# Gated linear attention by pairs of 128 tokens in place of chunks of 64 with carried states

## The reference

```
log_a = log_sigmoid(a_low @ w_a_up + b_a) / 16
b = cumsum(log_a within a chunk of 64 tokens)
q_d = q * exp(b);  k_d = k * exp(-b);  k_t = k * exp(b_last - b);  decay = exp(b_last)
att = tril(q_d @ k_d^T) per chunk;  o_intra = att @ v
for each chunk:  o_inter = q_d @ state;  state = decay * state + k_t^T @ v
o = rmsnorm(o_intra + o_inter) * silu(z)
```

## Time and profile before

| what | value |
|---|---|
| timed runs, median of 3 | 985.37 us |
| profiled execution, first to last instruction (span) | 984.4 us |
| time around the span (985.37 less 984.4) | 1.0 us |
| PE busy | 977.1 us, 99% |
| PE weight loads, beside the products | 828.7 us, 84% |
| DVE busy | 682.6 us, 69% |
| ACT busy | 585.1 us, 59% |
| POOL busy | 66.2 us, 7% |

### The profile page before, as it was taken

One profiled execution on the slowest core, in us unless ns is written; L12 is line 12 of the kernel. 1 busy time (PEld: TensorE's weight loads), 2 busy tenths in 40 slices (PEclk: granted clock), 3 DMA queues, 4 the chain that ended last, 5 costly groups with the idle time before them and its releaser, 6 DMA issues.

```text
span 984.4 us, 13450 instructions
## 1 busy us (share of the span) xinstructions
PE 977.1 (99%) x5186; PEld 828.7 (84%) x5186; DVE 682.6 (69%) x1159; ACT 585.1 (59%) x1026; POOL 66.2 (7%) x80
## 2 busy tenths in 40 slices
PE   9999999999999999999999999999999999999997
PEld 6887888888888998888888888888888777988886
DVE  5887776655667889766556678778577355787564
ACT  6777755444547896654445476557766354685443
POOL 1323110000000241000000000000020000000000
PEclk9999999999999999999999999999999999999999
DMA  9753555554555445555645556445533543336551
GB/s 364 308 195 129 171 174 211 198 205 175 200 185 173 170 161 181 177 208 174 227 177 200 185 196 248 171 171 190 195 129 137 186 148 128 129 129 208 179 190 43
DMA packets 27119, 180.33 MB, mean 183 GB/s; under 512 B 2992, under 2 KB 3888, under 8 KB 6320
## 3 DMA queue, kind: packets, MB, share of 16 engines
q1 hardware_dynamic: 26336, 176.98, 50.3%
q0 software_dynamic: 288, 2.10, 0.6%
q10 hardware_dynamic: 432, 0.39, 0.1%
HBM read 178.41 MB, written 1.05 MB: 182 GB/s over the span
## 4 chain that ended last, share of the span: by engine, by line
PE 99%; DMA 1%; DVE 0%; ACT 0%; SPq 0%; issue 0%; DVEq 0%
PE bank L340 25%; PE bank L295 16%; PE bank L297 16%; PE bank L296 16%; PE bank L348 13%; PE bank L310 1%; PE bank L470 1%; PE bank L486 1%; PE bank L591 1%; PE bank L520 1%; PE bank L311 1%; PE bank L531 1%; DMA front<-in_front 1%; PE bank L462 1%; PE bank L706 0%; PE bank L722 0%
## 5 line engine op out<-in xcount | busy, mean ns | idle before, releaser
L1357 DVE TENSOR_TENSOR lo<-raw,hi 128x1024 fp32r<-128x1024 f32 x318 | 375.9, 1228 | 20.0 <-ACT hi L837 20.0
L837 ACT ACTIVATE hi<-raw 128x1024 fp32r<-128x1024 f32 x318 | 320.2, 1050 | 96.9 <-PE bank L297 95.1
L340 PE MATMUL bank<-X,hi 128*128 128x512 f32 x1016 | 267.0, 395 | 0.0
L340 PEld LDWEIGHTS bank<-X,hi 128*128 128x128 f32 x1016 | 185.0, 189 | 33.2 <-issue 0.4
L348 PEld LDWEIGHTS bank<-X,lo 128*128 128x128 f32 x1016 | 138.5, 190 | 10.1
L348 PE MATMUL bank<-X,lo 128*128 128x256 f32 x1016 | 141.6, 282 | 0.0
L868 ACT ACTIVATE bt<-bank 128x256 f32<-128x256 f32 x135 | 51.0, 380 | 142.7 <-PE bank L340 134.3
L1371 DVE TENSOR_TENSOR zr<-bank,bt 128x256 f32<-128x256 f32 x64 | 27.1, 424 | 109.0 <-ACT bt L868 109.0
L295 PE MATMUL bank<-hi,zh 128*128 128x512 f32 x256 | 100.0, 391 | 0.0
L297 PE MATMUL bank<-hi,zl 128*128 128x512 f32 x256 | 99.8, 390 | 0.0
L296 PE MATMUL bank<-lo,zh 128*128 128x512 f32 x256 | 99.6, 389 | 0.0
(11 more groups left out here) (344 smaller groups left out, 1428.3 us busy)
## 6 DMA issues: line engine op xcount, KB each, us to landing
raw<-in_w SPq DMA_DIRECT2D x64, 1024.0 KB, 4.7
raw<-in_rin SPq DMA_DIRECT2D x8, 1024.0 KB, 4.7
raw<-in_wk SPq DMA_DIRECT2D x4, 1024.0 KB, 11.0
raw<-in_wq SPq DMA_DIRECT2D x4, 1024.0 KB, 9.4
raw<-in_wo SPq DMA_DIRECT2D x4, 1024.0 KB, 4.7
raw<-in_mk SPq DMA_DIRECT2D x4, 1024.0 KB, 4.8
raw<-in_mv SPq DMA_DIRECT2D x4, 1024.0 KB, 4.7
raw<-in_rout SPq DMA_DIRECT2D x4, 1024.0 KB, 4.8
```

The source lines that it names most:

```text
L340: return PE.matmul(bank[b][:, :], wh[:, c:c + P], x[:, k_, :, :].rearrange("p a b -> p (a b)"), start=k_ == 0, stop=k_ == NC - 1, skip_gro ...
L837: ACTE.activation(hi[u_ % HIS][:, c], raw[u_ % RAW][:, c], ACT.Copy).then_inc(hi_cut, 1)
L1357: DVE.tensor_tensor(lo[u_ % RAW][:, c], raw[u_ % RAW][:, c], hi[u_ % HIS][:, c].bitcast(F32), ALU.subtract).then_inc(lo_cut, 1)
```

## The change

The heads are worked in two halves of 128 tokens (the two rows of partitions) in place of four chunks of 64. The running sum starts anew every 128 tokens. The exponentials are taken relative to the sum at the middle of the half (token 63 of it), passed as a per-partition bias of the activation. The second half's tokens see the first half by one more score block (`gax`, 128 by 128), made from keys scaled to the first half's end and queries scaled from the second half's start. There are no states, no turned keys and no products on part of the array. PE does for a head: `g_first(n)`, three products of 128 columns; tile `ta` n; `g_second(n)`, three products of 256 columns; tile `wd` n. ACT makes six exponentials of 128 tokens for a head in place of two of 256 and copies the third score block; DVE makes two small scaled copies of the middles and ends, splits one scaling into halves, and masks the scores in two instructions that leave out one quarter, which two clears before the loop set to zero.

```diff
-            done = fill(("gkt", n), 1)
-            for j in range(2):
-                m = PE.transpose(bank[1][:, j * P:(j + 1) * P], gk[:, n, j * P:(j + 1) * P], ident[:, :])
-            m.then_inc(done, 1)
-        def g_states(n):
...
-            for c in (0, 2, 1):
-                r, j = (c % 2) * 64, c // 2
-                m = PE.matmul(bank[2 + c % 2][:, j * 256:j * 256 + 256], ktT[n % 2][r:r + 64, j, :],
-                              gv[r:r + 64, j, n * 256:(n + 1) * 256], start=True, stop=True, skip_group_check=True)
...
+            done = fill(("gax", n), 1)
+            PE.matmul(bank[1][:, 0:P], gk[:, n, 0:P], gk[:, n, P:S], start=True, stop=True).then_inc(done, 1)
...
-            for j in range(2):
-                PE.matmul(bank[3][:, j * 256:j * 256 + 256], at[n % 2][:, j, :], v_[:, j, :], start=j == 0, stop=False,
-                          skip_group_check=True)
-            for c in (2, 1, 3):
-                r, j = (c % 2) * 64, c // 2
-                m = PE.matmul(bank[3][r:r + 64, j * 256:j * 256 + 256], q_[:, c * 64:c * 64 + 64], st[c - 1][:, :],
-                              start=False, stop=True, skip_group_check=True)
+            PE.matmul(bank[3][:, 0:256], a_[:, 0, :], v_[:, 0, :], start=True, stop=False, skip_group_check=True)
+            PE.matmul(bank[3][:, 256:512], a_[:, 1, :], v_[:, 1, :], start=False, stop=False, skip_group_check=True)
+            PE.matmul(bank[3][:, 256:512], a_[:, 2, :], v_[:, 0, :], start=False, stop=True, skip_group_check=True).then_inc(done, 1)
...
             g_first(n)
             tokens("ta", n, X, (4, 5))
-            g_states(n)
+            g_second(n)
             tokens("wd", n, Y, (6, 7))
-            g_second(n)
...
-            ACTE.activation(tmp[n % 2][:, :], gb[:, n, :], ACT.Exp, scale=1.0 / 16).then_inc(ep_made, 1)
-            ACTE.activation(tmp[2 + n % 2][:, :], gb[:, n, :], ACT.Exp, scale=-1.0 / 16).then_inc(en_made, 1)
+            for j in range(2):
+                r = slice(j * P, (j + 1) * P)
+                i = ACTE.activation(tmp[n % 2][:, r], gb[:, n, r], ACT.Exp, scale=1.0 / 16, bias=dec[:, 1, n, 2 * j:2 * j + 1])
+            i.then_inc(ep_made, 1)
+            for j in range(2):
+                r = slice(j * P, (j + 1) * P)
+                i = ACTE.activation(tmp[2 + n % 2][:, r], gb[:, n, r], ACT.Exp, scale=-1.0 / 16, bias=dec[:, 0, n, 2 * j:2 * j + 1])
+            i.then_inc(en_made, 1)
+            ACTE.activation(sq[2 + n % 2][:, 0:P], gb[:, n, 0:P], ACT.Exp, scale=-1.0 / 16, bias=dec[:, 0, n, 1:2])
+            ACTE.activation(sq[2 + n % 2][:, P:S], gb[:, n, P:S], ACT.Exp, scale=1.0 / 16).then_inc(ex_made, 1)
...
-            ACTE.activation(ktT[n % 2][:, :, :], bank[1][:, 0:S].rearrange("p (a b) -> p a b", a=2),
-                            ACT.Copy).then_inc(freed[1], 1)
+            ACTE.activation(at[n % 2][:, 2, :], bank[1][:, 0:P], ACT.Copy).then_inc(freed[1], 1)
...
-            DVE.tensor_tensor_scan(gb[:, n, :], reset[:, :], u[:, :], 0.0, ALU.mult, ALU.add).then_inc(sum_made, 1)
+            step(DVE.tensor_tensor_scan(gb[:, n, :], reset[:, :], u[:, :], 0.0, ALU.mult, ALU.add))
+            own()
+            DVE.tensor_scalar(dec[:, 0, n, :], gb[:, n, 63:S:64], 1.0 / 16, None, ALU.mult)
+            DVE.tensor_scalar(dec[:, 1, n, :], gb[:, n, 63:S:64], -1.0 / 16, None, ALU.mult).then_inc(sum_made, 1)
...
-            d.wait_ge(ep_made, n + 1)
-            step(DVE.tensor_copy(dec[:, n, :], ep[:, 63:S:64]))
...
+            step(DVE.scalar_tensor_tensor(out=gk[:, n, P:S], in0=gq[:, n, P:S], scalar=128 ** -0.5, in1=ex[:, P:S],
+                                          op0=ALU.mult, op1=ALU.mult))
+            DVE.tensor_tensor(gk[:, n, 0:P], gk[:, n, 0:P], ex[:, 0:P], ALU.mult)
+            own()
+            d.wait_ge(ep_made, n + 1)
+            DVE.scalar_tensor_tensor(out=gq[:, n, :], in0=gq[:, n, :], scalar=128 ** -0.5, in1=ep[:, :], op0=ALU.mult,
+                                     op1=ALU.mult).then_inc(kd_made, 1)
...
-        def g_states(n):
-            d.wait_ge(*full["gu", n, 1])
-            if n:
-                d.wait_ge(*full["go", n - 1])
-            step(DVE.tensor_copy(st[0][:, :], bank[2][:, 0:256]))
...
-            DVE.scalar_tensor_tensor(out=st[2][:, :], in0=st[1][:, :], scalar=dec[:, n, 2:3], in1=bank[2][:, 256:512],
-                                     op0=ALU.mult, op1=ALU.add).then_inc(freed[2], 1)
...
-        "gmask": ((s <= t) & (s // 64 == t // 64)).astype(f),
-        "reset": np.tile((np.arange(S) % 64 != 0).astype(f), (P, 1)),
+        "gmask": (s <= t).astype(f),
+        "reset": np.tile((np.arange(S) % P != 0).astype(f), (P, 1)),
```

More of the change, by code:

```diff
@@ L122, in build @@
     score_read, mask_made, both_made = sem("score_read"), sem("mask_made"), sem("both_made")
-    w_made, sum_made, ep_made, en_made, kd_made = (
-        sem("w_made"), sem("sum_made"), sem("ep_made"), sem("en_made"), sem("kd_made"))
+    w_made, sum_made, ep_made, en_made, ex_made, kd_made = (
+        sem("w_made"), sem("sum_made"), sem("ep_made"), sem("en_made"), sem("ex_made"), sem("kd_made"))
     d_high, d_low, silu_made = sem("d_high"), sem("d_low"), sem("silu_made")
@@ L181, in build @@
     epsc = small("epsc", [1])
-    dec = small("dec", [4, 4])
+    dec = small("dec", [2, 4, 4])
     sp_ = small("sp_", [24])
@@ L239, in build @@
     og, szt = slot("og", 7, [2, D]), slot("szt", 8, [2, D])
-    at = [slot(f"at{i}", 9, [2, P], off=1024 * i) for i in range(2)]
-    ktT = [slot(f"ktT{i}", 9, [2, P], off=2048 + 1024 * i) for i in range(2)]
-    st = [slot(f"st{i}", 9, [256], off=4096 + 1024 * i) for i in range(3)]
+    at = [slot(f"at{i}", 9, [3, P], off=1536 * i) for i in range(2)]
     zx = slot("zx", 13)
@@ L694, in g_first @@
             m.then_inc(done, 1)
-            done = fill(("gkt", n), 1)
-            for j in range(2):
-                m = PE.transpose(bank[1][:, j * P:(j + 1) * P], gk[:, n, j * P:(j + 1) * P], ident[:, :])
-            m.then_inc(done, 1)
-        def g_states(n):
-            p.wait_ge(*free["gkt", n])
-            fill(("gu", n, 0), 2)
-            done = fill(("gu", n, 1), 3)
-            for c in (0, 2, 1):
-                r, j = (c % 2) * 64, c // 2
-                m = PE.matmul(bank[2 + c % 2][:, j * 256:j * 256 + 256], ktT[n % 2][r:r + 64, j, :],
-                              gv[r:r + 64, j, n * 256:(n + 1) * 256], start=True, stop=True, skip_group_check=True)
-                if c == 2:
-                    m.then_inc(filled[2], 1)
-            m.then_inc(done, 1)
+            done = fill(("gax", n), 1)
+            PE.matmul(bank[1][:, 0:P], gk[:, n, 0:P], gk[:, n, P:S], start=True, stop=True).then_inc(done, 1)
         def g_second(n):
             p.wait_ge(*free["gat", n])
-            p.wait_ge(*free["gu", n, 0])
+            p.wait_ge(*free["gax", n])
             done = fill(("go", n), 3)
-            v_, q_ = gv[:, :, n * 256:(n + 1) * 256], gq[:, n, :]
-            for j in range(2):
-                PE.matmul(bank[3][:, j * 256:j * 256 + 256], at[n % 2][:, j, :], v_[:, j, :], start=j == 0, stop=False,
-                          skip_group_check=True)
-            for c in (2, 1, 3):
-                r, j = (c % 2) * 64, c // 2
-                m = PE.matmul(bank[3][r:r + 64, j * 256:j * 256 + 256], q_[:, c * 64:c * 64 + 64], st[c - 1][:, :],
-                              start=False, stop=True, skip_group_check=True)
-            m.then_inc(done, 1)
+            v_, a_ = gv[:, :, n * 256:(n + 1) * 256], at[n % 2]
+            PE.matmul(bank[3][:, 0:256], a_[:, 0, :], v_[:, 0, :], start=True, stop=False, skip_group_check=True)
+            PE.matmul(bank[3][:, 256:512], a_[:, 1, :], v_[:, 1, :], start=False, stop=False, skip_group_check=True)
+            PE.matmul(bank[3][:, 256:512], a_[:, 2, :], v_[:, 0, :], start=False, stop=True, skip_group_check=True).then_inc(done, 1)
         def g_turn(n):
@@ L1202, in g_first @@
         def g_first(n):
-            a.wait_ge(*full["gkt", n])
+            a.wait_ge(*full["gax", n])
             if n >= 2:
                 a.wait_ge(*full["go", n - 2])
-            ACTE.activation(ktT[n % 2][:, :, :], bank[1][:, 0:S].rearrange("p (a b) -> p a b", a=2),
-                            ACT.Copy).then_inc(freed[1], 1)
+            ACTE.activation(at[n % 2][:, 2, :], bank[1][:, 0:P], ACT.Copy).then_inc(freed[1], 1)
         def g_second(n):
@@ L1743, in decay_sum @@
             own()
-            DVE.tensor_tensor_scan(gb[:, n, :], reset[:, :], u[:, :], 0.0, ALU.mult, ALU.add).then_inc(sum_made, 1)
+            step(DVE.tensor_tensor_scan(gb[:, n, :], reset[:, :], u[:, :], 0.0, ALU.mult, ALU.add))
+            own()
+            DVE.tensor_scalar(dec[:, 0, n, :], gb[:, n, 63:S:64], 1.0 / 16, None, ALU.mult)
+            DVE.tensor_scalar(dec[:, 1, n, :], gb[:, n, 63:S:64], -1.0 / 16, None, ALU.mult).then_inc(sum_made, 1)
         def decayed(n):
-            ep, en = tmp[n % 2], tmp[2 + n % 2]
```

(26 more changed lines are left out.)

## The result

The changed kernel takes 977.86 us (median of 4 runs, 977.05 to 978.24) against 985.38 us of the kernel before beside it. The ratio is 0.9922, 95% interval 0.991 to 0.9934: 7.5 us or 0.8% faster, between 6.5 and 8.9. The forecast was 977.2, its range 975.9 to 979.6.

A forecast was written before the change was run, and what follows sets the result against it. PE was taken to bound the kernel, its saved issue time coming off one for one: 16.0 less 7.8 saves 8.2, so span 984.4 becomes 976.2, with 1.0 around it 977.2 us against 985.37; range 975.9 to 979.6.

The forecast's parts named there:

- The sum on PE: Four heads: g_first, g_states, g_second and a 0.14 remainder cost 16.0 us before, 7.8 after; 8.2 saved.
- The pauses: Steps about 0.1 us too long beside products on 64 rows or columns, some 0.4 a head, counted as gone.
- Rival 1: Heads: pauses are the price of semaphore waits at stage borders and stay; 1.6 us given back, 978.8; chance 0.08.
- a bound of 1.6: Decay stretch: ACT's six exponentials of 128 cost 0.9 to 1.6 us more a head; 0.9 taken.
- the deepest exposure: Weight tile dz 2, low part: cover 5.6 us behind three heads' exponentials, against 4.8 at worst and 2.7 as taken.
- Cost 0: Decay stretch: added ACT and DVE work is hidden by cover and nothing reaches PE, 0 us.
- The moved `g_second`: Heads: it asks for at 5.5 us after g_first; DVE up to 1.3 late, cover over 3.
- rival 3: Decay stretch: exponentials with bias take 0.70 us each; 4.6 us given back, 981.8; chance 0.03.
- rival 4: At dz, PE is starved by ACT, slower if one exponential of 128 takes 1.01 us; 987.4; chance 0.02.
- Rival 2: Heads: moved g_second waits for at, some 1 us at each head; 4 us given back, 981.2; chance 0.05.

The follow-up runs named there:

- the first experiment: The changed kernel with g_second put back behind tile wd, the rest of the change kept: 977.67 us, ratio 0.9916 against the kernel before.
- the sister kernels: The changed kernel with two more exponentials a head on ACT (979.04 us), and with six more plus tile dz 2 in banks 2 and 3 (980.68 us).

## Why the prediction was right, point by point

**What bounds.** PE, one for one. Shown four times by added work (5.2, 5.0, 6.8 and 4.8 us of PE time gave 982.9, 983.1, 984.8 and 982.7, the last on another chip, where the first experiment stood at 977.7) and once by work taken away (10 us).

**The sum on PE.** Forecast 8.2, measured between like starts 8.0. The terms held to 0.01 or 0.02 us each: `g_first` 0.67 for 0.66 (770.62 to 771.75 less two steps), the new block as dear as two transposes, `g_second` 1.29 for 1.28. From the first L690 to the first L338 behind head 3 are 51.7 (770.85 to 822.52), for 51.5. The median fell by 7.5 only. The 0.7 between is inside the interval (6.5 to 8.9), and the first experiment, with the same work on PE, stood 8.5 below the kernel before on its chip. So the mechanism and the sum are confirmed by the trace; that the median fell within 0.7 of the forecast is partly luck, since the interval is wider than that.

**The pauses.** They went with the partial products: none is left in the changed kernel, none came with three full products at the same borders, and they came back with products on 64 rows or 64 columns. Rival 1 falls.

**ACT.** Six exponentials take from 677.10 to 678.76 in the rows below, 1.66 a head in place of 0.62 from start to start: 1.0 more, where I had 0.9 of a bound of 1.6. Each was to last 0.28. The biased ones last 0.39, which is what the row of L922 with 128 columns had (387 ns), and only the one without a bias 0.29. They overlap: a biased one starts 0.29 before the next, and that spacing is why the 0.9 held. ACT's timeline after the change, head 0:

```profile
677.10 0.68 ACT L1137 ACTIVATE tmp<-gb,dec 128x128 f32<-128x128 f32 x2
677.68 0.68 ACT L1141 ACTIVATE tmp<-gb,dec 128x128 f32<-128x128 f32 x2
678.27 0.39 ACT L1143 ACTIVATE sq<-gb,dec 128x128 f32<-128x128 f32 x1
678.56 0.29 ACT L1144 ACTIVATE sq<-gb 128x128 f32<-128x128 f32 x1
678.76 1.99 ACT L815 ACTIVATE hi<-raw 128x1024 fp32r<-128x1024 f32 x2
```

**The cover in the decay stretch: the size was wrong.** The step that failed is the sentence that the deepest exposure is the low part of `dz` 2, with 5.6 us. The tightest was a bank. `dz` 2 writes banks 4 and 5, and these come free when DVE has read `dz` 0, in its list behind the fourth head. After the change DVE's first read ends at about 695.2, and PE starts `dz` 2 one plain step after 696.48, at 696.7 (the first of that row's eight is the last of `dz` 1): 1.5 us are left. Four heads, not three, stand ahead of that read. "Cost 0" came out right, but with 1.5 us to spare. The cover of the low part, too, was used up otherwise than I had it. It went from 5.6 to 4.6 (the low part ends at 693.70, and its first products start at 698.33), and the bank's from 2.5 (694.88 to 697.35) to 1.5: 1.0 us each, where I had 2.7. The rest of ACT's longer work went into time in which ACT and DVE had been idle, such as a wait of ACT for PE of 1.29 before a copy of `gv`, which is gone. This idle time I had not looked for. With it used up, further work counts in full, as the experiments show: 0.6 us more a head already showed as a wait.

Rivals 3 and 4 named a price of 0.70 and 1.01 us for an exponential, which were to give back 4.6 and 10.2 us. Both went by the wrong cover. With six more of 0.29 a head, as if each of the six had taken twice its spacing or 0.58, the runs gave back 7.1, nearly the whole gain; rival 3's 4.6 would have needed some 0.5 and rival 4's 10.2 some 0.7 (estimates: 24 exponentials against a cover of 1.5, with the clock's part of 1.6 for rival 4). Their chances were still small, since the exponentials cost about what the rows said.

The place of the reads and of `dz` 2 before the change (DVE, then PE), and the low part of `dz` 2 after it (DVE, then the first products that read it):

```profile
694.46 1.14 DVE L1371 TENSOR_TENSOR sz<-bank,bt 128x256 f32<-128x256 f32 x3
697.12 2.00 PE L340 MATMUL bank<-X,hi 128*128 128x512 f32 x8
```

```profile
691.34 2.36 DVE L1342 TENSOR_TENSOR lo<-raw,hi 128x1024 fp32r<-128x1024 f32 x2
698.33 1.12 PE L346 MATMUL bank<-X,lo 128*128 128x256 f32 x8
```

DVE's timeline after, the last of head 3 and the two reads of `dz` 0, then PE's at the start of `dz` 2:

```profile
694.48 0.42 DVE L1747 SCALAR_TENSOR_TENSOR gq<-gq,tmp 128x256 f32<-128x256 f32 x1
694.82 0.75 DVE L1356 TENSOR_TENSOR sz<-bank,bt 128x256 f32<-128x256 f32 x2
```

```profile
696.48 2.00 PE L338 MATMUL bank<-X,hi 128*128 128x512 f32 x8
```

**The moved `g_second`.** Covered, as forecast, and worth nothing by itself. In head 2 DVE's scores start at 798.69, 2.0 after the start of their product (L690 at 796.69). Before the change it was 0.75 (801.97 after 801.22), so they are 1.25 later, where the forecast had up to 1.3. They end at 799.4, and PE reaches L701 at 802.85: 3.4 of cover, for "over 3". PE waits for no engine in the heads. Rival 2 falls.

```profile
798.69 0.41 DVE L1803 TENSOR_TENSOR at<-bank,gmask 64x256 f32<-64x256 f32 x1
799.12 0.29 DVE L1805 TENSOR_TENSOR at<-bank,gmask 64x128 f32<-64x128 f32 x1
...
802.85 0.59 PE L701 MATMUL bank<-gv,at 128*128 128x256 f32 x2
```

## What to carry to other kernels

Where one engine is busy in every slice, price a change by the starts of its instructions in that engine's timeline; here the end moved by that sum. Count cover for every thing the engine waits for: its inputs, but also the output bank it is to overwrite, whose reader may stand far down another engine's list. Look also for idle time of the other engines, which takes up some of their added work. Products on 64 rows gained here only by a neighbour on the other rows, and with their pauses three of them cost what three full ones did (1.26 and 1.29 us; 1.21 for three of 64 columns). The states they served were the work that could go.

## What was not expected of the hardware

Three float32 products of 64 rows on one row group took 1.69 us with their borders, more than three of 128 rows (1.29); on both row groups 1.26. After a wait of 5.4 us PE was granted 0.50 of its clock for some 3 us, which added about 1.6 us to the wait; after waits of 0.7 and 1.4 us in the sister kernels the seven L339 behind took 1.89 and 1.88, and the stretch behind the wait of 1.4 shows a granted clock of 1.00.
